# Sending the squares of a norm's last chunks straight to the matmul with ones, instead of adding them on VectorE first

## What is computed

```python
def rmsnorm(x, g):
    xf = x.astype(jnp.float32)
    y = xf * lax.rsqrt(jnp.mean(xf * xf, axis=-1, keepdims=True) + EPS)
    return (y * g.astype(jnp.float32)).astype(x.dtype)

def modulate(h, shift, scale):
    return h * (1 + scale) + shift

def first_block(x, c, ctx, ...):
    for l in range(DEPTH):
        h = modulate(rmsnorm(x, norm1_g[l]), sh1, sc1)
        ...
        x = x + g1 * gated_merge(p[..., QKV_END:], y_conv, y_attn, w_out[l])
        h2 = modulate(rmsnorm(x, norm2_g[l]), sh2, sc2)
        x = x + g2 * conv_ffn(h2, w_up[l], ffn_dw[l], ffn_dw_b[l], w_down[l])
        ...
    return rmsnorm(x, final_norm_g)

def second_block(x, meta, ...):
    for l in range(DEPTH):
        u = rmsnorm_2(h, norm_mix[l])
        ...
        h = h + jnp.concatenate([a_out, b_out, c_out], axis=-1) @ w_out[l]
        u = rmsnorm_2(h, norm_ff[l])
        h = h + jnp.square(jax.nn.relu(u @ w_ff1[l])) @ w_ff2[l]
    return rmsnorm_2(h, final_norm)[:, N_META:]
```

## Time and profile before

| | |
|---|---|
| median of three runs | 2203.66 us |
| the profiled execution's own time | 2212.03 us |
| its span, first to last instruction | 2210.3 us |
| TensorE busy | 2103.1 us (95%) |
| VectorE busy | 1027.6 us (46%) |
| ScalarE busy | 897.4 us (41%) |
| GpSimd busy | 1182.4 us (53%) |
| DVE additions into `rinv` at L1686 | 42, median 680 ns over three widths |
| TensorE's granted clock over the span | 0.967 |

### The profile page before, as it was taken

How to read it: one execution, slowest core, us unless ns; L and a number is a source line. 1 busy time by engine, 2 the same in 40 slices (tenths; PEclk the granted TensorE clock), 3 DMA queues, 4 the chain that set the end, 5 groups by cost and what they waited for, 6 DMA issues and landing times.

```text
span 2210.3 us, 34389 instructions
## 1 busy us (share of the span) xinstructions
PE 2103.1 (95%) x12568; PEld 1749.1 (79%) x12568; DVE 1027.6 (46%) x1940; ACT 897.4 (41%) x1521; POOL 1182.4 (53%) x904
## 2 busy tenths in 40 slices
PE   5999999999999999999999998999999989999997
PEld 2666666777888787877889987775999977759997
DVE  3077776544333226566767424245541043346401
ACT  3222434234333324345456544244454343345543
POOL 1333232425444553645769864631788846318885
PEclk8999999999999999999999999987999999979998
DMA  9798221336422231534446653321455543214663
GB/s 391 265 346 274 72 67 48 89 95 129 129 92 94 97 95 57 154 99 120 134 134 181 218 182 98 116 67 31 134 179 175 175 148 119 73 39 145 189 190 106
DMA packets 115686, 306.55 MB, mean 139 GB/s; under 512 B 29672, under 2 KB 44392, under 8 KB 115316
## 3 DMA queue, kind: packets, MB, share of 16 engines
q1 hardware_dynamic: 112664, 298.06, 42.0%
q10 hardware_dynamic: 2908, 6.90, 1.7%
HBM read 300.19 MB, written 8.06 MB: 139 GB/s over the span
## 4 chain that ended last, share of the span: by engine, by line
issue 41%; POOL 36%; PE 20%; DVE 2%; POOLq 0%; ACT 0%; DMA 0%; DVEq 0%
POOL w_lo L575 36%; PE bank L1063 5%; PE bank L1064 4%; PE bank L1065 4%; PE bank L1464 1%; PE bank L1465 1%; PE bank L1466 1%; PE bank L1663 1%; PE bank L1628 0%; DVE nb L1686 0%; PE bank L1627 0%; PE bank L1670 0%; PE bank L1668 0%; PE bank L1666 0%; DVE u_lo L1694 0%
## 5 line engine op out<-in xcount | busy, mean ns | idle before, releaser
L575 POOL TENSOR_TENSOR w_lo<-raw,w_hi 128x512 fp32r<-128x512 f32 x884 | 1166.1, 1345 | 1006.4 <-ACT w_hi L616 1005.9
L616 ACT ACTIVATE w_hi<-raw 128x1024 fp32r<-128x1024 f32 x442 | 465.9, 1055 | 316.7 <-PE bank L1065 248.9
L1063 PE MATMUL bank<-h_hi,w_hi 128*128 128x512 f32 (+1 forms) x1216 | 426.4, 351 | 11.7 <-DVE h_lo L1694 7.2
L1065 PE MATMUL bank<-h_hi,w_lo 128*128 128x512 f32 (+1 forms) x1216 | 417.9, 344 | 0.0
L1064 PE MATMUL bank<-h_lo,w_hi 128*128 128x512 f32 (+1 forms) x1216 | 417.9, 344 | 0.0
L1063 PEld LDWEIGHTS bank<-h_hi,w_hi 128*128 128x128 f32 x1216 | 231.4, 190 | 68.6 <-issue 27.9
L1063 PE MATMUL bank<-u_hi,w_hi 128*128 128x272 f32 (+1 forms) x880 | 260.8, 296 | 11.0 <-POOL w_lo L575 4.2
L1064 PE MATMUL bank<-u_lo,w_hi 128*128 128x272 f32 (+1 forms) x880 | 256.6, 292 | 0.0
L1065 PE MATMUL bank<-u_hi,w_lo 128*128 128x272 f32 (+1 forms) x880 | 256.0, 291 | 0.0
L1065 PEld LDWEIGHTS bank<-h_hi,w_lo 128*128 128x128 f32 x1216 | 231.3, 190 | 29.7
L1064 PEld LDWEIGHTS bank<-h_lo,w_hi 128*128 128x128 f32 x1216 | 231.6, 190 | 28.5 <-issue 0.2
(11 more groups left out here) (283 smaller groups left out, 3623.0 us busy)
## 6 DMA issues: line engine op xcount, KB each, us to landing
raw<-in_wstream SPq DMA_DIRECT2D x442, 512.0 KB, 3.5
ada_raw<-in_wada SPq DMA_DIRECT2D x96, 512.0 KB, 6.6
biash<-rpb_by_offset SPq DMA_DIRECT2D x64, 64.0 KB, 3.5
rpb_by_offset<-in_rpb SPq DMA_DIRECT2D x16, 224.0 KB
bias_by_distance<-vec ACTq DMA_DIRECT2D x1, 3264.0 KB
bias<-bias_by_distance SPq DMA_DIRECT2D x2, 1632.0 KB, 8.8
X<-in_x_in ACTq DMA_DIRECT2D x1, 2048.0 KB, 11.7
bias<-bias_by_distance SPq DMA_DIRECT2D x2, 864.0 KB, 6.4
```

The source lines that it names most:

```text
L575: i = pool.tensor_tensor(w_lo[:, s, part], raw[:, s, part], w_hi[:, s, part].bitcast(F32), ALU.subtract)
L616: act.activation(w_hi[:, s, :], raw[:, s, :], ACT.Copy).then_inc(sem("w_hi_ready"), 1)
L1063: pe.matmul(o, hi, a_hi, start=start, stop=False)
L1065: return pe.matmul(o, lo, a_hi, start=False, stop=stop)
```

## The change

The function `n_late` says how many of the last chunks are late: 4 for 512 tokens, else 3. VectorE no longer adds the squares of late chunks; TensorE first multiplies the total of the early ones, then each late square, into the same bank. In the norms whose squares end with the sum in `rinv`, ScalarE's square of chunk c (which overwrites the buffer of chunk c - 2) then waits for TensorE's matmul of chunk c - 2 where that one is late: chunks 6 and 7 with 512 tokens, chunk 7 with fewer. The numbers of idle matmuls ahead shrink (N1 4 to 2, N2 13 to 5, N3 6 to 2, N4 and N5 9 to 5), and in N2, N4 and N5 one is put ahead of each late square's matmul but the last (`gap=1`).

```diff
+        def n_late(T):
+
+            return 4 if T == T_BOTH else 3
...
                     if c >= (2 if summed else 3):
-                        act.wait_ge(*after("norm_summed" if summed else "norm_added", (tag, c - 2)))
+                        by_pe = summed or c - 2 >= DC - n_late(T)
+                        act.wait_ge(*after("norm_summed" if by_pe else "norm_added", (tag, c - 2)))
...
-            def norm_sum(tag, T, summed=True, before=(0, 0), behind=0, reader="norm_root", total=rinv):
+            def norm_sum(tag, T, summed=True, before=(0, 0), behind=0, reader="norm_root", total=rinv, gap=0):
...
                 claim(4)
+                alone = 0 if summed else DC - 1 if total is not rinv else DC - n_late(T) - 1
                 if not summed:
-                    pe.wait_ge(*after("norm_added", (tag, DC - 1)))
-                    pe.matmul(aux[0][:, 0:T], ones_d, total[:, 0:T], start=True, stop=True)\
-                        .then_inc(*done("norm_summed", (tag, DC - 1)))
-                for c in range(DC if summed else 0):
+                    pe.wait_ge(*after("norm_added", (tag, alone)))
+                    mm = pe.matmul(aux[0][:, 0:T], ones_d, total[:, 0:T], start=True, stop=alone == DC - 1)
+                    if alone == DC - 1:
+                        mm.then_inc(*done("norm_summed", (tag, DC - 1)))
+                for c in range(0 if summed else alone + 1, DC):
+                    if gap and c < DC - 1:
+                        keep_busy(before[0], gap)
                     pe.wait_ge(*after("norm_sq", (tag, c)))
-                    pe.matmul(aux[0][:, 0:T], ones_d, sq[:, c % 2, 0:T], start=c == 0, stop=c == DC - 1)\
+                    pe.matmul(aux[0][:, 0:T], ones_d, sq[:, c % 2, 0:T], start=summed and c == 0, stop=c == DC - 1)\
                         .then_inc(*done("norm_summed", (tag, c)))
...
-                    norm_sum((layer, 1), T_BOTH, False, (0, 13), 15)
+                    norm_sum((layer, 1), T_BOTH, False, (0, 5), 15, gap=1)
...
-                norm_sum((layer, 2), T, False, (7, (4, 6)[layer]), (13, 8)[layer])
+                norm_sum((layer, 2), T, False, (7, 2), (13, 8)[layer])
...
-                    norm_sum(("fin", 1), SEQ, False, (0, 9), 6)
+                    norm_sum(("fin", 1), SEQ, False, (0, 5), 6, gap=1)
...
-                    norm_sum((layer, 3), T2, False, (0, 9), 10)
+                    norm_sum((layer, 3), T2, False, (0, 5), 10, gap=1)
...
             def norm_add(tag, c, T, total=rinv):
+                if total is rinv and c >= DC - n_late(T):
+                    return
```

## The result

The changed kernel takes 2210.48 us (median of 20 runs, 2204.80 to 2221.55) against 2204.43 (median of 20, 2200.14 to 2211.20) for the kernel before, run beside it: a ratio of 1.0030, 95% interval 1.0018 to 1.0042. By this ratio it is 6.6 us slower (4.0 to 9.3), by the two medians 6.05. Forecast were 5.4 us slower, 2209.1 us, in a range of 2205.9 to 2212.4.

A forecast was written before the change was run, and what follows sets the result against it. TensorE is busy nearly throughout, so only the six norms' stretches count. Terms 3.45 + 0.53 + 0.28 + 0.65 + 0.74 - 0.22 = +5.4 us on the median 2203.66 give 2209.1 us, range 2205.9 to 2212.4.

The forecast's parts named there:

- N1: Norm behind `mix`, 512 columns: square 6 waits for TensorE, then roundings, square 7 and table load queue on ScalarE; +3.45 us.
- N2: Norm of 512 columns with 13 idle matmuls before: TensorE's stream now sets the end, table load hides; +0.53 us.
- N3: Norm of 256 columns: slow VectorE additions gone, but ScalarE's later start eats the gain; +0.28 us.
- N4: Norm where the total waits for addition 4 and square 7 starts later, at 1315.60 instead of 1314.95; +0.65 us.
- N5: Norm worked out in the same way as N4; +0.74 us.
- The rival that only the matmuls count: At N1: roundings cost nothing, +1.8 instead of +3.45 us, total 2207.4 us; chance 0.19, shared with other terms short by as much.
- 0.94, and three times 0.44 + 0.94: TensorE's stream in N2: the total's matmul 0.94 us, then three times an idle matmul 0.44 and a matmul 0.94.
- N6: Norm without idle matmuls, which waited for its matmul before; -0.22 us.
- The clock rival: Clock halves behind N3, N4 and N5, 1.65 us each: one gives 2210.7 us, all three 2214.0; chance 0.22.
- The faster rival: In the norms, squares don't wait and the removed additions were the bound; -5.0 us, 2198.7 us; chance 0.09.

The follow-up runs named there:

- experiment 2: Changed kernel with own buffers for late squares, so none waits for TensorE; against the kernel before, ratio 1.0003 (0.9989 to 1.0018).
- N1 taken back: Changed kernel, but N1 has no late chunks and its four idle matmuls again; ratio to the kernel before 1.0006 (0.9993 to 1.0019).
- experiment 1: Two edits of the changed kernel, N1 taken back and N1 alone; ratios to the kernel before 1.0006 and 1.0005.
- N1 alone: Changed kernel with late chunks only at N1, other norms with their old idle matmuls; ratio to the kernel before 1.0005 (0.9993 to 1.0018).
- experiment 3: Changed kernel with the rounding between squares 6 and 7 of N1 put ahead of square 6; N1 6.59 us for 7.19, single execution 2217.16 us.

## Why the prediction came out right

**Direction and size.** The range held, and the forecast of +5.4 us lies between what the six norms add up to in the trace (4.4) and what the runs give (6.6, interval 4.0 to 9.3). The 2.2 us between these two aren't explained. The interval covers them, and only one execution of each kernel was traced, so a further cost outside the norms is neither shown nor excluded. That the forecast came as close to the runs as it did is in part luck: its terms were 1.0 us too high against the norms, and the runs lie above the norms.

**N1** carried the sum as forecast, +3.19 for +3.45. Its working held step by step: square 6 released by the matmul of square 4, then the queue without a gap, root 7.19 us (forecast 7.4) behind the first idle matmul. The rival that only the matmuls count was priced at +1.8; alone they measured +1.35 (experiment 2), but the roundings did not hide. The order of a strict queue decided between the two, as argued.

**N2** was mis-sized most: the step "0.94, and three times 0.44 + 0.94". In a stream the matmul of 512 columns took 0.86 us (859.10 to 859.96) and the idle one 0.43: a step is 1.29 us, not 1.38. The 0.94, which the prediction calls that of a stream, was read at the one pair 471.89 to 472.83, where TensorE had stood idle for 0.73 us before the matmul; the one in a stream here was quicker. Up to the start of the last matmul that is 4 x 0.08 us for the matmuls and 8 x 0.01 for the idle ones; and from that start, 862.97 + 0.86, to the root it was 1.06 us, not 1.14. Together these are the 0.48 us. N1 and N3 were overpriced in the same way, by some 0.1 us each: at N1 square 6 started 2.84 us behind the first idle matmul, forecast were 2.96, and ScalarE's queue took 4.35 us from there instead of 4.49 (0.95 instead of 1.06 from the rounding to square 7); at N3 square 7 started at 1.98 instead of 2.09.

**N4, N5 and N6** came within 0.06 us of their terms. The direct wait behind the last square, 1.73 us to the root, held to the hundredth (1318.49 to 1320.22).

**Table load and root.** Behind a table load of 1.28 us the root starts at once: at N4 the load ends at 1320.21 and the root starts at 1320.22. There is no further time for the drain of 1.38 us that the Trainium skill (ScalarE: Activation LUTs, "What ACT_TABLE_LOAD costs") puts to it; the measurement decides. With it N2's root would have come 1.2 us later than it did (863.45 + 1.28 + 1.38 = 866.1, an estimate from that figure, for 864.89).

**The clock rival** fell as far as one trace of the changed kernel shows it: N3's stretch is where it could have struck (busy 1.94 of 4.00 us, less than the 2.32 of 3.40 ahead of the half clock behind N1; the gap was the 2 us that the prediction worked out), and the granted clock stayed at 1.00, 2.4 GHz, there and in the 20 us behind it. The Trainium skill (TensorE: Matmul & The Clock Gate, "HAM oscillation") holds gaps in TensorE's work to be a cause of such a fall; this gap brought none. The prediction said that the row behind N1 bears this out, and that is more than the traces carry: behind the same gap at N1 the clock fell in the kernel before and stayed full with N1 taken back (experiment 1). What these traces show is that a fall came behind such a gap in some executions and not in others; where it came it cost 1.5 us, for the 1.65 at most that the prediction put to it.

**The faster rival** ("the squares don't wait, and the additions were the bound") was false of this change, since the squares do wait, but its mechanism is real. Given buffers of its own, N3 gained 1.16 us (priced 1.2, though its own 1109.7 less 1108.6 makes 1.1) and N6 0.93 (1.0); N2 gained 1.5 us (priced 2.0) only once four idle matmuls, one ahead of its stream and the three between the squares, went too.

## What to carry to other kernels

Work handed to another engine takes its buffer's release with it: ask which engine's queue the next writer now waits for, and what stands behind that writer in its own strict queue. Price a chain of like instructions from the distance of two in a stream, and keep the latency to the waiting engine for the last one alone. Where single executions differ by as much as the edit is worth, measure the interval from the last useful instruction to the first of the next stage, and let only the sum be judged by many runs.

## What was not expected of the hardware

- The spread. The same 450 us of work between N4 and N5 took 450.1 us in the changed kernel and 450.6 with N1 taken back, both at a mean granted clock of 0.94, with 51 us at half clock. It took 454.2 and 454.3 us in the kernel before and in N1 alone, both at 0.93, with 61 us at half clock. These four would fit the late chunks at N4 as the cause, which the first two have and the last two lack. But the kernel of experiment 3, whose N4 is that of the changed kernel, took 454.6 us at 0.93, with 61 us at half clock. So the edit at N4 alone doesn't set it; what does stays open.
- The table load can be moved by a square root of one column: the squares and roundings behind it ran on without a second load, and the root gained up to 1.40 us (N3, 4.66 to 3.26).
- The slow additions at N3, two of 256 columns in 3.10 us, did limit that norm, and vanish with the change. The trace of before shows what ran beside them, GpSimd's subtractions for `w_lo`:

```profile
1104.47 2.51 POOL L575 TENSOR_TENSOR w_lo<-raw,w_hi 128x512 fp32r<-128x512 f32 x2 [0.31 <-ACT w_hi L616]
...
1107.31 2.67 POOL L575 TENSOR_TENSOR w_lo<-raw,w_hi 128x512 fp32r<-128x512 f32 x2 [0.33 <-ACT w_hi L616]
```

  Taken singly, the additions took 1.51 and 1.48 us, and each ended 0.28 to 0.29 us behind the end of the subtraction that was running when it began (1106.98 to 1107.27, 1108.57 to 1108.85). Two of the seven additions at N4 took 1.00 and 1.10 us in the same way (1310.64 to 1310.92, 1312.06 to 1312.34); the other five, with no subtraction beside them, took the 0.41 to 0.43 that the prediction gives for all. So the slow ones seem to have waited for GpSimd; no run took the subtractions away, and the cause isn't shown.
